# Five broadcasts of the tokens' norms by TensorE: one fp32 product each, or two products of rounded diagonals and their rests; and one token sum moved behind the norm's chain

## The chip, the cores and the metric

The kernel runs on one core of one Trainium2 chip. The time is the device time of one execution of the whole program, in microseconds (us). The trace is one execution of the program taken by the hardware profiler; every start time below counts from the start of its span.

## The reference

Two transformer blocks follow one another on 512 tokens of width 1024, with 16 meta tokens ahead of them, all in fp32. What matters for this change is the norm that stands ahead of each large product:

```python
def rms_norm(x, g):
    xf = x.astype(jnp.float32)
    y = xf * lax.rsqrt(jnp.mean(xf * xf, axis=-1, keepdims=True) + EPS)
    return (y * g.astype(jnp.float32)).astype(x.dtype)
...
hn = rms_norm(h, ffn_norm_g[l])
h = h + (jax.nn.silu(hn @ w_ffn_gate[l]) * (hn @ w_ffn_up[l])) @ w_ffn_down[l]
```

The first block has a windowed attention and an indexed sparse latent attention (its queries pass a norm of 256 entries), gates, an output product and a feed-forward part of 2816. The second has a differential and a windowed attention, gates, an output product and a feed-forward part of the same size. A norm closes each block.

## The kernel before

Activations lie transposed: partitions are features, the 512 tokens are columns. A large product takes a pair of output chunks (`b` = 0 and 1, banks `psL[:, 0]` and `psL[:, 1]`) at a time. Every fp32 weight tile is loaded into `stage`, rounded by ScalarE to float32r (`wh`, line 805) and its rest is made by VectorE (`wl = stage - wh`, line 1250, functions `low` and `low_next`); activations are split into `hn[:, 0]` and `hn[:, 1]` in the same way. TensorE then takes three products for each of the eight chunks `k` of the features: `wh` by high part, `wh` by rest, `wl` by high part (line 2106, function `product`). A product of pair `i`, side `b` starts when the rest of its weights is there (`lo[b]`) and when its bank has been read for pair `i-1` (`ev[b]`).

Each engine runs its own list of instructions in order, written out by hand, and waits on semaphores. The argument `between={(m, k): f}` of `product` puts other TensorE work ahead of chunk `k` of part `m`.

The factor of the norm of a token, 1/rms, is not applied to `hn` before the product but to the product's result, as a tile `R` in which every partition holds the 512 factors. It is made by a chain that crosses two engines:

- TensorE adds the squares over partitions (`sums`, line 2167: products with one column of ones), result in `psT[:, 1, 0:4]`, tokens on partitions; semaphore `ssq_mm`.
- VectorE computes 1/sqrt in one `tensor_scalar` and eight steps on 4 columns (`new_rms`, lines 1698 and 1275 to 1282), and `diagonals` (line 1292) multiplies the identity by the factors of each of the four token blocks: four 128x128 instructions into `diag`; semaphore `diag_ok`.
- TensorE multiplies `diag` by a matrix of ones (`spread_rms`, line 2171), one fp32 product of 512 columns, which puts the factors into every partition of a bank of `psT`; semaphore `bcast`. The trace has two MATMUL records for one fp32 product.
- VectorE copies the bank to `R` (line 1774; 1904 and 1905 in the second block's start), semaphore `R_ok`.

Such a broadcast stands in six places: in `kv1` (`spread_first`), ahead of the latent queries (`spread_second`, inside `product("aq1", 1, 1)`), in each of the two feed-forward parts (`norm_spread`, inside `product("gu1a", 0, 1)` and `product("gu2a", 0, 1)`), and two at once at the start of the second block (`spread_both`, inside `product("kv2", 0, 1)`, ahead of chunk 1 of its second part; the products of kv2 have 264 columns). The second of that pair takes `diag2`, which lies in `tmp[:, 0]`.

In `swiglu` VectorE's order at the first pair of a feed-forward part is

```python
low(name, i, 1)
token_sum(l, 0)
new_rms(head[0])
diagonals(diag, rs[:, 0:4]).then_inc(diag_ok, 1)
low_next(name, i, False)
v.wait_ge(bcast, head[1])
v.tensor_copy(R, psT[:, 1, :]).then_inc(R_ok, 1)
...
v.tensor_tensor(ft[:, 0, :], psL[:, 0, :], R, ALU.mult).then_inc(ev[0], 1)
```

`token_sum(l, 0)` (line 1708) is one 128x1024 subtraction on the normed activations, which ScalarE rounds later and the fast form of the gate products reads in later pairs. The last line (line 1783) frees bank 0 for the product of the second pair. On entry to `aq1`'s last product the bank was freed by `take_scaled("aq1", 0, 1, ...)` (line 1387), which VectorE runs behind `diagonals` and two instructions for the latent queries' rest (line 1468). In `kv2` bank 0's pair is freed by `take_keys` (line 1383), which needs `R`.

Of the kernel before, what the change touches and what calls it, by code (L numbers as in the profile page):

```python
# [21 lines left out]
F32 = mybir.dt.float32  # L22
F32R = mybir.dt.float32r
# [3 lines left out]
ALU = mybir.AluOpType  # L27
AX_X = mybir.AxisListType.X

P = 128  # L30
# [4 lines left out]
NB = SEQ // P  # L35
# [229 lines left out]
def build(nc, t, out):  # L265
    with ExitStack() as ctx:
# [8 lines left out]
        def at(name, shape, offset, dt=F32):  # L275

            n = int(np.prod(shape[1:])) * size[dt]
            assert offset + n <= nc.sbuf_usable_end, (name, offset + n - nc.sbuf_usable_end)
            return nc.alloc_sbuf_tensor_at(name, shape, dt, offset=offset), -(-(offset + n) // 32) * 32

        def keep(name, shape, dt=F32):
            tensor, top[0] = at(name, shape, top[0], dt)
            return tensor
# [5 lines left out]
        wl = keep("wl", [P, 2, NFH * P], F32R)  # L289
        Rk = keep("Rk", [P, NKEY])  # L290
        R = Rk[:, META:NKEY]
        tmp = keep("tmp", [P, 2, SEQ])
        ident = keep("ident", [P, P])
        ones = keep("ones", [P, P])
        gvec = keep("gvec", [P, NROWS])
        bhalf = keep("bhalf", [P, 2 * KD])
        g12 = keep("g12", [P, KD])
# [85 lines left out]
        tail = max(o, ar0 + 4 * (2 * NFH * SEQ + 6 * SEQ + 3 * 4 * SEQ))  # L383
        qT, o = at("qT", [P, 4, SEQ], tail)
        selm, _ = at("selm", [P, NB, NKEY], o, BF16)
        diag, o6 = at("diag", [P, NB, P], o)
        sq, o6 = at("sq", [P, SEQ], o6)
        sqacc, _ = at("sqacc", [P, 2, SEQ], tail)
        hotA, o5 = at("hotA", [BUCKETS + 1, LEN_A], tail)
# [241 lines left out]
        def _(pool):  # L631
# [9 lines left out]
                                        pattern=[[META, NH]], channel_multiplier=-1))  # L641
            own.link(pool.memset(tab[BUCKETS:BUCKETS + 1, :], NEG))
            own.link(pool.memset(st[:, 0, 0:6], 1.0))
            pool.memset(ones[:], 1.0).then_inc(consts, 1)
            pool.wait_ge(consts, 1)
            for tile_ in (cn, ikn, avn):
                pool.memset(tile_[:, MC, :], 0.0)
# [589 lines left out]
        def _(v):  # L1237
# [6 lines left out]
            def low(name, i, b, by_pool=POOL_LOW):  # L1244

                if name in by_pool:
                    return
                v.wait_ge(hi[b], PAIR0[name] + i + 1)
                n = KC[name] * P
                v.tensor_tensor(wl[:, b, 0:n], stage[:, b, 0:n], wh[:, b, 0:n].bitcast(F32), ALU.subtract).then_inc(lo[b], 1)  # L1250
# [18 lines left out]
            def rsqrt(x, y, n, parts=P, done=None):  # L1269
# [16 lines left out]
                else:  # L1286
                    dv.link(ins)

            def diagonals(dst, r):

                for n in range(NB):
                    ins = v.tensor_scalar(dst[:, n, :], ident[:], r[:, n:n + 1], None, ALU.mult)
                return ins
# [166 lines left out]
            v.wait_ge(ssq_mm, 1)  # L1460
            dv.link(v.tensor_scalar(st[:, 7, 0:4], psT[:, 1, 0:4], 1.0 / 256, EPS, ALU.mult, ALU.add))
            rsqrt(st[:, 7, 0:4], rs[:, 0:4], 4)
            diagonals(diag, rs[:, 0:4]).then_inc(diag_ok, 1)

            v.wait_ge(bqhi, 2)
            for k in range(2):
# [228 lines left out]
            def new_rms(ssq_count, n0=0, n1=NB, done=None):  # L1695

                v.wait_ge(ssq_mm, ssq_count)
                dv.link(v.tensor_scalar(st[:, 8, n0:n1], psT[:, 1, n0:n1], 1.0 / D, EPS, ALU.mult, ALU.add))
                rsqrt(st[:, 8, n0:n1], rs[:, n0:n1], n1 - n0, done=done)
# [63 lines left out]
            def swiglu(l, part, head=None):  # L1763
                name, f0, pairs_ = f"gu{l}{'abc'[part]}", before_part(l, part), gate_pairs(l, part)
                first, pair0 = pairs_[0]
                for i in range(first):
                    if i == 0:
                        low(name, i, 1)
                        token_sum(l, 0)
                        new_rms(head[0])  # L1770
                        diagonals(diag, rs[:, 0:4]).then_inc(diag_ok, 1)
                        low_next(name, i, False)
                        v.wait_ge(bcast, head[1])
                        v.tensor_copy(R, psT[:, 1, :]).then_inc(R_ok, 1)
                        v.wait_ge(R_ok, head[1])
                    elif i == 1:
                        token_sum(l, 1)
                    elif i == 2:
                        token_sum_low(l, 1)
                    elif i == 3:  # L1780
                        token_sum_low(l, 3)
                    done(name, i, 0)
                    v.tensor_tensor(ft[:, 0, :], psL[:, 0, :], R, ALU.mult).then_inc(ev[0], 1)  # L1783
                    if i:
                        low_next(name, i, False)
                    opened(i, f0, ft[:, 0, :], ft[:, 1, :])
                    if i == 1:
                        token_sum_low(l, 0)
                        token_sum(l, 2)
                    elif i == 2:  # L1790
                        token_sum(l, 3)
                        token_sum_low(l, 2)
                    elif i == first - 1:
                        weight_sums(name, first, pair0)
                        sum_low(pair0, 0)
                        second_low(name, first)
                    times_up(name, i, 1, i, f0, ft[:, 0, :], (lambda: low(name, i + 1, 1)) if i < first - 1 else None)
                    if i == first - 1:
                        sum_low(pair0, 1)
                    inner_low(i, f0)  # L1800

                for i, n in pairs_:
                    last = i == pairs_[-1][0]
                    done(name, i, 0)
                    v.wait_ge(out_x, 2 * n + 1)
                    v.tensor_tensor(ft[:, 0, 0:HT], psS[:, 1, 0:HT], part_x[:, 0:HT], ALU.add).then_inc(ev[0], 1)
                    low(name, i + 1, 0)
                    low(name, i + 1, 1)
                    v.wait_ge(acc_y, 2 * n + 2)
                    v.wait_ge(out_x, 2 * n + 2)  # L1810
                    dv.link(v.tensor_tensor(ft[:, 0, HT:], psS[:, 2, 0:HT], part_x[:, HT:], ALU.add))
                    v.tensor_tensor(ft[:, 0, :], ft[:, 0, :], R, ALU.mult).then_inc(gate_ok, 1)
                    v.wait_ge(acc_x, 3 * n + 3)
                    v.wait_ge(out_y, n + 1)
                    v.wait_ge(out_z, n + 1)
                    v.tensor_tensor(ft[:, 2, :].rearrange("p (a t) -> p a t", a=2), psS[:, 0, 0:HT].unsqueeze(1).broadcast_to([P, 2, HT]),
                                    part_z[:].rearrange("p (a t) -> p a t", a=2), ALU.add).then_inc(ev[1], 1)
                    v.wait_ge(ev[1], PAIR0[name] + i + 1)
                    v.tensor_tensor(ft[:, 2, :], ft[:, 2, :], R, ALU.mult).then_inc(gate_ok, 1)
                    v.wait_ge(gate_ok, 2 * n + 2)  # L1820
                    opened(i, f0, ft[:, 0, :], ft[:, 1, :])
                    opened(i + 1, f0, ft[:, 2, :], tanh2[:])
                    if not last:
                        weight_sums(name, i + 2, n + 1)
                    times_up(name, i, 0, i + 1, f0, ft[:, 0, :])
                    low_next(name, i + 1, last)
                    if not last:
                        sum_low(n + 1, 0)
                    inner_low(i, f0)
                    if not last:  # L1830
                        sum_low(n + 1, 1)
                    times_up(name, i + 1, 1, i + 1, f0, ft[:, 2, :])
                    if not last:
                        second_low(name, i + 2)
                    elif part == 2:
                        low(f"dn{l}c", 0, 1)
                    inner_low(i + 1, f0)
# [57 lines left out]
            dv.link(v.tensor_scalar(st[:, 9, 0:4], st[:, 9, 0:4], 1.0 / D, EPS, ALU.mult, ALU.add))  # L1895
            rsqrt(st[:, 9, 0:4], rs[:, 4:8], 4)
            dv.link(v.tensor_tensor(rs[:, 8:12], rs[:, 0:4], rs[:, 4:8], ALU.mult))
            diag2 = tmp[:, 0, :].rearrange("p (n c) -> p n c", n=NB)
            diagonals(diag, rs[:, 0:4])
            diagonals(diag2, rs[:, 8:12]).then_inc(diag_ok, 1)  # L1900
            low_next("kv2", 0, False)
            v.wait_ge(bcast, 4)
            v.tensor_copy(Rk[:, 0:META], Rmeta[:, 1, :])
# [181 lines left out]
        def _(pe):  # L2085
# [84 lines left out]
            def spread_rms(bank, d):  # L2170
                return pe.matmul(psT[:, bank, :], ones[:], d.rearrange("p n c -> p (n c)"), start=True, stop=True)


            pe.wait_ge(consts, 1)
            pe.wait_ge(g1_in, 16)
# [67 lines left out]

            def spread_second():
                pe.wait_ge(diag_ok, 2)
                spread_rms(1, diag).then_inc(bcast, 1)

            def logits(t):

# [201 lines left out]
            def layer_rest(l, ssq0, norm):  # L2451
# [16 lines left out]

                def norm_spread():
                    pe.wait_ge(diag_ok, ssq0 + 1)  # L2470
                    spread_rms(1, diag).then_inc(bcast, 1)

                product(name, 0, 0, hn, made=(hg_lo, KD * (2 * l - 2)))
                product(name, 0, 1, hn, between={(0, 1): norm_sums, (0, 6): norm_spread})
# [16 lines left out]

            def spread_both():
                pe.wait_ge(diag_ok, 4)
                spread_rms(0, diag)
                spread_rms(1, tmp[:, 0, :].rearrange("p (n c) -> p n c", n=NB)).then_inc(bcast, 1)

            product("kv2", 0, 0, hn, meta=3, made=(hg_lo, KD), between={(1, 2): sums_of_both})
            product("kv2", 0, 1, hn, meta=1, between={(1, 1): spread_both})
            products("kv2", hn, first=1, meta=1)
            product("qa2", 0, 0, hn)  # L2500
            for b in range(2):
# [186 lines left out]
```

## Time and profile before

| | |
|---|---|
| three runs | 1478.28, 1479.45 and 1480.2 us, median 1479.45 |
| the profiled execution | 1478.32 us, its span 1476.6 us |
| TensorE (PE) busy | 1462.8 us, 99% of the span |
| VectorE (DVE) busy | 957.4 us, 65% |
| ScalarE (ACT) busy | 609.1 us, 41% |
| GpSimd (POOL) busy | 178.9 us, 12% |

A busy matmul includes an end that is modelled: successive MATMUL records of one engine overlap, and the distance of two starts is what one of them takes of the engine. "Idle before, releaser" names the time for which an engine's next instruction waited and what ended the wait.

### The profile page before, as it was taken

The numbers are of one execution on the slowest core, as the hardware profiler recorded it, in microseconds if no ns is written. First come the engines' busy times: TensorE is split into PE (matmuls) and PEld (weight loads), VectorE is DVE, ScalarE is ACT, GpSimd is POOL, SyncE is SP. The second block draws the span as 40 slices with busy tenths as digits, with TensorE's granted clock in tenths as the row PEclk, the third lists the DMA queues.
The fourth block names the chain that finished last, engine by engine and source line by source line (L and its number), as shares of the span: only waits on it lengthen the run. The fifth ranks groups of instructions, "written<-read, shape, count | busy, mean of one in ns | idle before, by whom it ended". The sixth has DMA issues, their size and how long they took to land.

```text
span 1476.6 us, 21866 instructions
## 1 busy us (share of the span) xinstructions
PE 1462.8 (99%) x8042; PEld 1229.8 (83%) x8042; DVE 957.4 (65%) x1736; ACT 609.1 (41%) x1066; POOL 178.9 (12%) x163
## 2 busy tenths in 40 slices
PE   8999999999999999999999999999999999999998
PEld 7867786888888898898898777777888888988987
DVE  6678986575784587387854472524757955873875
ACT  5234446535442343244511364444344423432444
POOL 2013325100000000000003663220000000000000
PEclk9999999999999999999999999999999999999999
DMA  7624320133333333332323202221333333333322
GB/s 178 152 78 144 112 57 1 32 111 99 93 100 95 113 101 86 99 115 74 98 86 85 57 5 82 58 65 36 114 90 96 100 101 114 91 95 100 115 71 101
DMA packets 250325, 132.99 MB, mean 90 GB/s; under 512 B 21241, under 2 KB 247669, under 8 KB 250238
## 3 DMA queue, kind: packets, MB, share of 16 engines
q1 hardware_dynamic: 248014, 123.92, 29.3%
q0 software_dynamic: 2144, 7.77, 1.9%
q8 instruction: 55, 0.90, 0.2%
q14 instruction: 32, 0.26, 0.1%
q10 hardware_dynamic: 80, 0.14, 0.0%
HBM read 129.67 MB, written 6.38 MB: 92 GB/s over the span
## 4 chain that ended last, share of the span: by engine, by line
PE 95%; DVE 2%; ACT 1%; DMA 1%; issue 1%; POOL 0%; DVEq 0%; ACTq 0%; SPq 0%
PE psL L2106 52%; PE psS L2129 12%; PE psL L2292 12%; PE psS L2106 5%; PE psT L2301 2%; PE psL L2427 1%; PE psS L2605 1%; PE psS L2342 1%; PE psL L2560 1%; PE psS L2400 1%; PE psS L2583 1%; PE psS L2531 1%; PE psS L2329 1%; DMA stage<-in_w_out 1%; PE psS L2532 0%
## 5 line engine op out<-in xcount | busy, mean ns | idle before, releaser
L805 ACT ACTIVATE wh<-stage 128x1024 fp32r<-128x1024 f32 (+3 forms) x231 | 224.8, 973 | 381.6 <-PE psL L2106 270.1
L2106 PE MATMUL psL<-hn,wh 128*128 128x512 f32 x1104 | 343.6, 392 | 0.4 <-DVE ft L1783 0.4
L1250 DVE TENSOR_TENSOR wl<-stage,wh 128x1024 fp32r<-128x1024 f32 (+2 forms) x188 | 208.3, 1108 | 77.0 <-ACT wh L805 76.8
L2106 PEld LDWEIGHTS psL<-hn,wh 128*128 128x128 f32 x1104 | 204.7, 188 | 45.7 <-issue 4.8
L2106 PE MATMUL psL<-hn,wl 128*128 128x512 f32 x552 | 215.0, 389 | 0.0
L2106 PE MATMUL psL<-hid,wh 128*128 128x512 f32 x680 | 209.4, 389 | 0.0
L2292 PE MATMUL psL<-hn,wh 128*128 128x512 f32 x496 | 165.0, 414 | 0.2 <-DVE yn L1991 0.2
L2106 PEld LDWEIGHTS psL<-hid,wh 128*128 128x128 f32 x680 | 127.5, 188 | 26.8
L2106 PE MATMUL psL<-hid,wl 128*128 128x512 f32 x340 | 132.3, 389 | 0.0
L2106 PEld LDWEIGHTS psL<-hn,wl 128*128 128x128 f32 x552 | 103.6, 188 | 21.9
L668 POOL TENSOR_TENSOR wl<-stage,wh 128x1024 fp32r<-128x1024 f32 (+1 forms) x43 | 97.5, 2270 | 197.8 <-ACT wh L805 197.8
L2292 PEld LDWEIGHTS psL<-hn,wh 128*128 128x128 f32 x496 | 84.4, 189 | 23.9 <-issue 11.1
L2292 PE MATMUL psL<-hn,wl 128*128 128x512 f32 x248 | 97.8, 394 | 0.0
L1842 DVE TENSOR_TENSOR hT<-hT,psL 128x512 f32 (+1 forms) x46 | 31.6, 686 | 85.3 <-PE psL L2106 85.2
L2106 PE MATMUL psS<-hn,wh 128*128 128x264 f32 x448 | 83.7, 288 | 0.3 <-DVE hn L1300 0.2
L2106 PE MATMUL psL<-mix,wh 128*128 128x512 f32 x256 | 79.8, 393 | 0.3 <-DVE wl L1250 0.2
L2129 PE MATMUL psS<-xt,wsh 128*128 128x256 f32 x432 | 79.3, 283 | 0.0
L2106 PEld LDWEIGHTS psL<-hid,wl 128*128 128x128 f32 x340 | 63.8, 188 | 13.1
L2106 PEld LDWEIGHTS psS<-hn,wh 128*128 128x128 f32 x448 | 70.0, 190 | 2.2 <-issue 1.2
L2129 PEld LDWEIGHTS psS<-xt,wsh 128*128 128x128 f32 x432 | 67.4, 192 | 0.0
L2106 PE MATMUL psS<-hn,wl 128*128 128x264 f32 x224 | 63.8, 285 | 0.0
L2129 PE MATMUL psS<-xt,wsl 128*128 128x256 f32 x216 | 61.1, 283 | 0.0
(443 smaller groups left out, 2565.2 us busy)
## 6 DMA issues: line engine op xcount, KB each, us to landing
stage<-in_w_in SPq DMA_DIRECT2D x53, 512.0 KB, 3.7
stage<-in_w_ffn_gate SPq DMA_DIRECT2D x22, 512.0 KB, 3.7
stage<-in_w_ffn_up SPq DMA_DIRECT2D x22, 512.0 KB, 3.7
stage<-in_w_ff_gate SPq DMA_DIRECT2D x22, 512.0 KB, 3.6
stage<-in_w_ff_up SPq DMA_DIRECT2D x22, 512.0 KB, 3.7
stage<-in_w_out SPq DMA_DIRECT2D x16, 512.0 KB, 3.9
stage<-in_w_ffn_down SPq DMA_DIRECT2D x16, 512.0 KB, 3.9
stage<-in_w_ff_down SPq DMA_DIRECT2D x16, 512.0 KB, 3.9
```

The source lines that it names most:

```text
L668: pool.tensor_tensor(wl[:, b, 0:n], stage[:, b, 0:n], wh[:, b, 0:n].bitcast(F32), ALU.subtract).then_inc(lo[b], 1)
L805: act.activation(wh[:, b, 0:n], stage[:, b, 0:n], ACT.Copy).then_inc(hi[b], 1)
L1250: v.tensor_tensor(wl[:, b, 0:n], stage[:, b, 0:n], wh[:, b, 0:n].bitcast(F32), ALU.subtract).then_inc(lo[b], 1)
L1842: v.tensor_tensor(hT[:, n, :], hT[:, n, :], psL[:, b, :], ALU.add).then_inc(ev[b], 1)
L2106: ins = pe.matmul(dst, w[:, b, k * P:(k + 1) * P], x[:, part, k, c0:c1], start=k + n == 0, stop=k == kc - 1 and n == 2)
L2129: ins = pe.matmul(dst, w[:, cols], x(part, k), start=not add and k + n == 0, stop=k == KD // 2 - 1 and n == 2, skip_group_check=True)
L2292: ins = pe.matmul(psL[:, b, :], w[:, b, k * P:(k + 1) * P], hn[:, part_, k, META:], start=k + n == 0, stop=k == KD - 1 and n == 2)
L2301: ins = pe.transpose(psT[:, n % 2, m * P:(m + 1) * P], tile[:, col:col + P], ident[:])
L2329: pe.matmul(psS[:, 2 * (u % 2), 0:W], aqT[r, h % 4, i * P:(i + 1) * P], akz[r, k0:k0 + W], start=True, stop=True).then_inc(p["s"], 1)
L2342: ins = pe.matmul(psS[:, 2 * (i % 2) + 1, h * HD:(h + 1) * HD], PTa[:, u % 2, n * P:(n + 1) * P], avn[:, c, h // 4 * HD:h // 4 * HD + HD], ...
L2400: ins = pe.matmul(latent_banks(u0 + g)[:, bank, 0:k1 - k0], qT[r, t % 4, i * P:(i + 1) * P], kz[r, t % 4, k0:k1], start=True, stop=True)
L2427: ins = pe.matmul(psL[:, i % 2, h * HD:(h + 1) * HD], PT[:, n % 4, m * P:(m + 1) * P], vB[:, c, h * HD:(h + 1) * HD], start=h == 0 and m = ...
```

## The change

Five of the six broadcasts (all but the one in `kv1`) take two float32r products in place of one fp32 product. `diagonals_split` first writes the four rounded diagonals, and then, behind a wait on the engine's own semaphore, their four rests by `scalar_tensor_tensor` (identity times factor minus the rounded value). The matrix of ones is now made as float32r: a memset of `junk` and a copy behind it. `diag2_r` takes the place of all of `tmp`, and `diag_r` is twice as long as `diag` was. In `swiglu` the first token sum stands behind the diagonals. In `kv2` the two broadcasts stand ahead of chunk 6 of the second part, not ahead of chunk 1.

```diff
-            pool.memset(ones[:], 1.0).then_inc(consts, 1)
+            own.link(pool.memset(junk[:, 0:P], 1.0))
+            pool.tensor_copy(ones_r[:], junk[:, 0:P]).then_inc(consts, 1)
...
+            def diagonals_split(dst, r):
+
+                for n in range(NB):
+                    ins = v.tensor_scalar(dst[:, 0, n, :], ident[:], r[:, n:n + 1], None, ALU.mult)
+                dv.link(ins)
+                for n in range(NB):
+                    ins = v.scalar_tensor_tensor(out=dst[:, 1, n, :], in0=ident[:], scalar=r[:, n:n + 1], in1=dst[:, 0, n, :].bitcast(F32),
+                                                 op0=ALU.mult, op1=ALU.subtract)
+                return ins
...
-            diagonals(diag, rs[:, 0:4]).then_inc(diag_ok, 1)
+            diagonals_split(diag_r, rs[:, 0:4]).then_inc(diag_ok, 1)
...
                         low(name, i, 1)
+                        new_rms(head[0])
+                        diagonals_split(diag_r, rs[:, 0:4]).then_inc(diag_ok, 1)
                         token_sum(l, 0)
-                        new_rms(head[0])
-                        diagonals(diag, rs[:, 0:4]).then_inc(diag_ok, 1)
                         low_next(name, i, False)
...
-            diag2 = tmp[:, 0, :].rearrange("p (n c) -> p n c", n=NB)
-            diagonals(diag, rs[:, 0:4])
-            diagonals(diag2, rs[:, 8:12]).then_inc(diag_ok, 1)
+            diagonals_split(diag_r, rs[:, 0:4])
+            diagonals_split(diag2_r, rs[:, 8:12]).then_inc(diag_ok, 1)
...
+            def spread_split(bank, d):
+                for part in range(2):
+                    ins = pe.matmul(psT[:, bank, :], ones_r[:], d[:, part].rearrange("p n c -> p (n c)"), start=part == 0, stop=part == 1)
+                return ins
...
-                spread_rms(1, diag).then_inc(bcast, 1)
+                spread_split(1, diag_r).then_inc(bcast, 1)
...
-            product("kv2", 0, 1, hn, meta=1, between={(1, 1): spread_both})
+            product("kv2", 0, 1, hn, meta=1, between={(1, 6): spread_both})
```

## Rows read from the trace of the kernel before

**Rows 1.** The page: TensorE's clock in 40 slices, and all engines' busy time

```profile
PE 1462.8 (99%) x8042; PEld 1229.8 (83%) x8042; DVE 957.4 (65%) x1736; ACT 609.1 (41%) x1066; POOL 178.9 (12%) x163
...
PEclk9999999999999999999999999999999999999999
```

**Rows 2.** Waits of TensorE: waiter, releaser; us in total, times, longest

```profile
PE psL L2106 <- DVE ft L1783: 0.4, 2, 0.2
```

**Rows 3.** Timeline of TensorE in gu1a: start, length, engine, line, operation

```profile
381.33 0.39 PE L2106 MATMUL psL<-hn,wl 128*128 128x512 f32 x1
...
382.01 0.39 PE L2106 MATMUL psL<-hn,wl 128*128 128x512 f32 x1
...
383.55 0.40 PE L2106 MATMUL psL<-hn,wl 128*128 128x512 f32 x1
...
384.25 0.40 PE L2106 MATMUL psL<-hn,wl 128*128 128x512 f32 x1
384.86 0.70 PE L2106 MATMUL psL<-hn,wh 128*128 128x512 f32 x2 [0.22 <-DVE ft L1783]
385.39 0.39 PE L2106 MATMUL psL<-hn,wl 128*128 128x512 f32 x1
```

**Rows 4.** Timeline of VectorE in gu1a

```profile
376.67 1.22 DVE L1708 TENSOR_TENSOR ta<-hg 128x1024 f32<-128x1024 f32 x1
378.94 0.16 DVE L1698 TENSOR_SCALAR st<-psT 128x4 f32<-128x4 f32 x1 [1.05 <-PE psT L2167]
...
380.72 0.88 DVE L1292 TENSOR_SCALAR diag<-ident,rs 128x128 f32<-128x128 f32 x4
381.52 1.22 DVE L1250 TENSOR_TENSOR wl<-stage,wh 128x1024 fp32r<-128x1024 f32 x1
383.30 0.69 DVE L1774 COPY Rk<-psT 128x512 f32<-128x512 f32 x1 [0.56 <-PE psT L2171]
384.02 0.69 DVE L1783 TENSOR_TENSOR ft<-psL,Rk 128x512 f32<-128x512 f32 x1
```

**Rows 5.** Timeline of both engines around `spread_second`

```profile
82.36 1.41 DVE L1468 SCALAR_TENSOR_TENSOR bqg<-bqT,gvec,bqg 128x512 fp32r<-128x512 f32 x2
...
83.68 0.68 DVE L1387 SCALAR_TENSOR_TENSOR aqT<-psL,Rk 128x512 f32<-128x512 f32 x1
...
84.28 0.36 DVE L1481 SCALAR_TENSOR_TENSOR acc<-relu,iwn,causal 128x144 f32<-128x144 f32 x1
...
84.89 0.62 PE L2106 MATMUL psL<-hn,wh 128*128 128x512 f32 x2
...
87.15 1.02 PE L2171 MATMUL psT<-diag,ones 128*128 128x512 f32 x2
```

**Rows 6.** Timeline of both engines around `spread_both` in kv2

```profile
737.12 0.87 DVE L1292 TENSOR_SCALAR tmp<-ident,rs 128x128 f32<-128x128 f32 x4
...
737.41 0.28 PE L2106 MATMUL psS<-hn,wl 128*128 128x264 f32 x1
...
740.07 0.17 DVE L1903 COPY Rk<-Rmeta 128x16 f32<-128x16 f32 x1 [0.94 <-PE psT L2171]
740.11 0.28 PE L2106 MATMUL psS<-hn,wl 128*128 128x264 f32 x1
...
741.47 0.71 DVE L1383 TENSOR_TENSOR kaT<-psS,Rk 128x528 f32<-128x528 f32 x1
...
742.30 0.28 PE L2106 MATMUL psS<-hn,wl 128*128 128x264 f32 x1
```

**Rows 7.** Timeline of TensorE at the start of the program

```profile
3.06 0.25 PE L2176 MATMUL psT<-ident,rows 8*128 8x8 f32 x1 [3.06 <-POOL ones L644]
4.62 1.97 PE L2199 MATMUL psL<-ident,xin 128*128 128x128 f32 x8 [1.31 <-DMA xin<-in_x]
```

**Rows 8.** Windows: length, busy us and instructions of each engine, PEclk, DMA, GB/s

```profile
9.00:12.00 3.00, 2.32 (x17) 1.98 (x16) 2.96 (x6) 3.00 (x7) 0.39 (x1) 0.83 1.11 353
12.00:13.90 1.90, 1.90 (x10) 1.68 (x9) 1.86 (x4) 1.90 (x6) 1.90 (x4) 0.50 0.38 68
```

More of the change, by code:

```diff
@@ L291, in build @@
         R = Rk[:, META:NKEY]
+        diag2_r, _ = at("diag2_r", [P, 2, NB, P], top[0], F32R)
         tmp = keep("tmp", [P, 2, SEQ])
         ident = keep("ident", [P, P])
-        ones = keep("ones", [P, P])
+        ones_r = keep("ones", [P, P], F32R)
+        ones = ones_r[:].bitcast(F32)
         gvec = keep("gvec", [P, NROWS])
@@ L385, in build @@
         selm, _ = at("selm", [P, NB, NKEY], o, BF16)
-        diag, o6 = at("diag", [P, NB, P], o)
+        diag, _ = at("diag", [P, NB, P], o)
+        diag_r, o6 = at("diag_r", [P, 2, NB, P], o, F32R)
         sq, o6 = at("sq", [P, SEQ], o6)
@@ L2470, in norm_spread @@
                     pe.wait_ge(diag_ok, ssq0 + 1)
-                    spread_rms(1, diag).then_inc(bcast, 1)
+                    spread_split(1, diag_r).then_inc(bcast, 1)
                 product(name, 0, 0, hn, made=(hg_lo, KD * (2 * l - 2)))
@@ L2493, in spread_both @@
                 pe.wait_ge(diag_ok, 4)
-                spread_rms(0, diag)
-                spread_rms(1, tmp[:, 0, :].rearrange("p (n c) -> p n c", n=NB)).then_inc(bcast, 1)
+                spread_split(0, diag_r)
+                spread_split(1, diag2_r).then_inc(bcast, 1)
             product("kv2", 0, 0, hn, meta=3, made=(hg_lo, KD), between={(1, 2): sums_of_both})
-            product("kv2", 0, 1, hn, meta=1, between={(1, 1): spread_both})
+            product("kv2", 0, 1, hn, meta=1, between={(1, 6): spread_both})
             products("kv2", hn, first=1, meta=1)
```

## The prediction

> **What bounds the kernel now.** I read the page first. TensorE is busy for 99% of the span and its granted clock is full in all 40 slices, while VectorE stands at 65% [rows 1]. So a microsecond taken off TensorE's own work is worth a microsecond, and so is each one for which TensorE is made to wait; an average of 65% on VectorE says nothing about one chain on it. The second view was the list of TensorE's waits. The reader is to see that TensorE already waits for the line just behind a broadcast (line 1783, the first product by `R`), twice [rows 2], once in each feed-forward part. Then I read the timelines of both engines around each of the five places.
>
> **What two rounded products save.** In gu1a a group of three rounded products takes 382.01 - 381.33 = 0.68 us, 0.227 us each [rows 3]. The group with the broadcast in it takes 383.55 - 382.01 = 1.54 us, so the fp32 broadcast takes 0.86 us of TensorE. Two rounded products of the same 512 columns take 0.45. The saving is 0.41 us a place, 2.0 us for five. The bounds: nothing, if a product by ones cost what an fp32 pass does (0.43), and 0.41; I take 0.41, since the same form of product stands 0.68 us beside it.
>
> **What the split costs on VectorE.** The four `tensor_scalar` stay (0.88 us together [rows 4]). Added are a wait on the engine's own semaphore and four `scalar_tensor_tensor` of 128 columns. None of this size is in the trace. The nearest takes 0.36 us for 144 columns [rows 5], and 16 columns fewer make about 0.345. Two instructions of this kind in a row, with no wait between them, end 1.41 us after the first begins [rows 5]; the second starts some 0.67 us behind the first, so an instruction begins about 0.07 us before the one ahead ends, and the step is 0.27. The gap of a wait is 383.30 + 0.69 to 384.02, 0.03 us [rows 4]. Estimate: 0.03 + 3 x 0.27 + 0.345 = 1.19 us a split, both until its semaphore and until the next instruction. Bounds: the step of the `tensor_scalar`, (0.88 - 0.28) / 3 = 0.20, gives 0.82; four that each wait for the one before, 4 x 0.40, give 1.6.
> The Trainium skill ("VectorE: DVE Perf Modes", the section on the TRN2 errata) says that each SBUF-source instruction pays a fixed latency, so many small tiles lose most, which speaks against four more small ones; its table gives 58 cycles plus one per column, 0.194 us at 0.96 GHz. By that figure the four add about 0.78 us, and the whole forecast would be some 2 us lower; the row of 0.36 us for 144 columns is well above its 0.21.
>
> **gu1a and gu2a.** Before, the token sum (1.22 us) ran from 376.67 to 377.89 and VectorE then stood idle for 1.05 us until TensorE's sums came, so the norm's chain starts at 378.94 in any order [rows 4]: ahead of the chain the token sum was free. Behind it, it is not. The new order by these rows:
> - the rounded diagonals end at 381.60, the rests at 382.79;
> - TensorE comes to the broadcast at 382.24, waits until about 382.85, runs 0.45 us and loses 0.1 on restarting: it is at the end of side 1 (two groups of 0.68 further) at about 384.75. Before it was there at 384.25 + 0.23 = 384.48;
> - token sum 382.71 to 383.93, then the rest of the next weights (`low_next`) 383.97 to 385.18, then the copy to `R` from 385.11 (the broadcast is long done), then line 1783 from 385.83 to 386.52.
>
> TensorE needs line 1783 for pair 1, and took it up 0.15 us after it ended: 384.86, with a pair that was 0.70 long instead of 0.61 [rows 3, 4]. It now takes it up at 386.67. The shift is 1.81 us. The same as a sum: token sum 1.26, split 1.19, less the 0.64 for which VectorE used to wait for the broadcast. The saving of 0.41 vanishes in TensorE's wait, which grows from about 0.4 to about 1.9. What is queued behind: ScalarE's tanh, the product for side 1 and all of the pair, all of which wait for line 1783 anyway and move with it. SP's load for pair 2 is issued behind `low_next`, 2.4 us later, and its slot is wanted only at the end of a product of 5.5 us; I cost it at nothing. Two places: +3.6 us, bounds +2.9 and +4.4 by the step.
>
> **kv2.** The last of the two diagonals ended at 737.99 [rows 6]. With two splits in the chain it is 740.37. The broadcasts' new place is five chunks further on; a chunk is (742.30 - 740.11) / 6 = 0.365 us, so TensorE is there at 737.53 + 1.82 = 739.35 and waits 1.05 us, instead of some 0.5 before. Four rounded products and the restart take 1.0, and the bank is whole, with its modelled tail, at about 741.6. Before it was at 740.03. From the first copy (740.07) to the end of `take_keys` (741.47 + 0.71 = 742.18) are 2.11 us, all in a row [rows 6]; now they run from 741.64 to 743.75. TensorE, which took up the next product at 742.30 + 0.12 = 742.42 without waiting, has only two chunks of cover left, arrives at 742.15 and starts at about 744.0 with the restart: +1.6 us. In other words, the later place keeps the diagonals' lateness off TensorE and pays it back at `take_keys`. Bounds: +0.9 and +2.4.
>
> **spread_second.** The broadcast itself stands at 87.15, the diagonals were done before 82.44 [rows 5], so no wait there and 0.41 is saved. But `take_scaled` (83.68, ends 84.36) is behind the diagonals on VectorE and frees the bank for TensorE's product at 84.89 [rows 5]: a cover of 0.53 less 0.15 for the semaphore. With 1.19 more it ends at 85.55, and TensorE starts at 85.70 and loses 0.09 on restarting: +0.9. Net +0.5, bounds +0.1 and +0.9.
>
> **The start.** The matrix of ones is two GpSimd instructions, so the first transpose at 3.06 comes some 0.35 us later (one more short instruction and a wait; none of GpSimd's shown is dearer at this size); it is 0.25 long, and TensorE then waited for x until 4.62 [rows 7]. That 1.31 us hides it: 0. With the cover gone it would be 0.35.
>
> **Sum.** 0.5 + 3.6 + 1.6 = +5.7 us. The profiled execution, 1478.32 us (1476.6 of span, 1.7 around it), becomes 1484.0. It lay 1.1 us below the median of the runs, so against the median: 1485.1 us. Terms at their bounds give 0.1 + 2.9 + 0.9 = 3.9 and 0.9 + 4.4 + 2.4 = 7.7, so 1483.3 to 1487.2, and the runs spread by about 1 us either way.
>
> **Rivals.**
> - *The chain hides after all* (not slower). VectorE has slack where I see none, and only TensorE's side is left: -2.0 us, 1477.4; if the two waits for line 1783 went too, 1476.5. It decides at one point, whether line 1783 ends by 384.33 (TensorE's arrival 384.48 less 0.15). It already ended 0.4 us later than that, and 1.8 is put ahead of it. Chance 0.07.
> - *Half is given back.* A later wait of TensorE in the pairs that follow shrinks because everything it waits for did not shift, weights from memory above all. The rows show no wait of TensorE for a weight load, so little is there to give back. About 1482. Chance 0.1.
> - *Rounded by ones is no cheaper than an fp32 pass* (the change doesn't do what it says). The feed-forward places do not move, since VectorE sets them; spread_second and kv2 get 0.4 and 0.8 dearer: 1486.3. Against it stand the steps of rows 3. Chance 0.03.
> - *The clock falls in the longer waits.* From 9 to 12 us, where TensorE was busy for 2.32 of 3 us with short transposes and waits, the granted clock went to 0.83 of full, and then to 0.50 for 1.9 us [rows 8]: about 2.9 us at the lower level, 1.5 us lost. If each of the three waits of 1 to 2 us brought that on, +4.5: 1489.6. Against it: those waits lie between dense products. The Trainium skill ("TensorE: Matmul & The Clock Gate", the section on HAM oscillation) warns that idle gaps between bursts of matmuls bring the 1.2 GHz level back; rows 8 show the level, no row here shows a lone gap doing it. Chance 0.04.
>
> **How the numbers follow.** My case has 0.76. The range is 1482.0 to 1488.0: the bounds of the terms with 1 us of spread below and above, which takes in the third rival and half of the second; outside are the first, the fourth and the rest, under 0.2. A measurement can tell about 0.2%, 3.0 us, from no change. Slower by more than that (above 1482.4) are my case, the third and fourth rivals and a little of the second: 0.84. Within it are most of the second, and the first where the two waits stay: 0.12. Faster needs more than the whole saving of 2.0: 0.04.
>
> **What the profile after would show.** The product at line 2106 that opens pair 1 of gu1a and gu2a idles some 1.7 to 2 us for line 1783, `take_keys` becomes a releaser of TensorE (about 1.6 us), and `take_scaled` in aq1 one with about 0.7. The broadcast's records are 0.39 long and 0.23 apart. The rests are about 0.345 long, 0.27 apart. In gu1a the broadcast waits about 0.5 us for the rests. I am wrong if the rests take under 0.15 us apiece, if the copy to `R` begins within 1 us of the broadcast in gu1a, or if the added idle time in these four places sums to less than 3 us.

## The result and the profile after

The changed kernel takes 1484.53 us (median of 7 runs, 1484.19 to 1485.44); the kernel before takes 1479.45 (7 runs, 1478.28 to 1481.19). The ratio is 1.0033, 95% interval 1.0024 to 1.0043: slower by 5.1 us, where 5.7 was forecast. The profiled execution of the changed kernel has a span of 1482.4 us against 1476.6.

First the page: busy time, share of the span and instructions of each engine.

```profile
PE 1463.0 (99%) x8042; PEld 1231.6 (83%) x8042; DVE 963.0 (65%) x1756; ACT 609.2 (41%) x1066; POOL 179.2 (12%) x164
```

Beside [rows 1] VectorE has 20 instructions and 5.6 us more, at an unchanged share of 65%. TensorE's share stays at 99% too, though its idle time (span less busy time) went from 13.8 to 19.4 us. Where the loss lies the page doesn't say. The waits of TensorE do (waiter, releaser; us in total, times, longest):

```profile
PE psL L2119 <- DVE ft L1797: 3.4, 2, 1.7
...
PE psT L2188 <- DVE diag_r L1299: 1.6, 3, 0.9
PE psS L2119 <- DVE kaT L1397: 1.5, 1, 1.5
...
PE psL L2119 <- DVE aqT L1401: 0.6, 1, 0.6
```

Line 1797 is line 1783 of before, 1397 is `take_keys` and 1401 `take_scaled`. The first wait was 0.4 us in all [rows 2], the last two were not in the list, and the second was one of 0.4 in kv2. The new waits name the four places of the forecast. (The 3.4 us for `ones` and 1.0 us for x, which are in the list too, belong to the start of the program.)

The instructions on the split diagonals (duration in ns, least, median and most):

```profile
L1296 DVE TENSOR_SCALAR diag_r<-ident,rs x20: 277/281/288, 82.0 to 1124.2; 128x128 fp32r<-128x128 f32 x20
L1299 DVE SCALAR_TENSOR_TENSOR diag_r<-ident,rs,diag_r x20: 341/344/352, 82.9 to 1125.3; 128x128 fp32r<-128x128 f32 x20
...
L2188 PE MATMUL psT<-diag_r,ones x10: 393/398/502, 88.4 to 1126.1; 128*128 128x512 f32 x10
```

One of the four instructions that make the rests takes 0.344 us (0.345 was estimated from the 144-column row).

gu1a, VectorE's timeline (start, length, engine, line, operation), beside [rows 4]:

```profile
379.49 0.16 DVE L1712 TENSOR_SCALAR st<-psT 128x4 f32<-128x4 f32 x1 [2.11 <-PE psT L2180]
...
381.27 0.88 DVE L1296 TENSOR_SCALAR diag_r<-ident,rs 128x128 fp32r<-128x128 f32 x4
382.18 1.14 DVE L1299 SCALAR_TENSOR_TENSOR diag_r<-ident,rs,diag_r 128x128 fp32r<-128x128 f32 x4
383.23 1.22 DVE L1722 TENSOR_TENSOR ta<-hg 128x1024 f32<-128x1024 f32 x1
384.49 1.23 DVE L1254 TENSOR_TENSOR wl<-stage,wh 128x1024 fp32r<-128x1024 f32 x1
385.63 0.69 DVE L1788 COPY Rk<-psT 128x512 f32<-128x512 f32 x1
386.35 0.69 DVE L1797 TENSOR_TENSOR ft<-psL,Rk 128x512 f32<-128x512 f32 x1
```

and TensorE's, beside [rows 3]:

```profile
382.63 0.39 PE L2119 MATMUL psL<-hn,wl 128*128 128x512 f32 x1
383.37 0.73 PE L2188 MATMUL psT<-diag_r,ones 128*128 128x512 f32 x2 [0.35 <-DVE diag_r L1299]
...
385.09 0.39 PE L2119 MATMUL psL<-hn,wl 128*128 128x512 f32 x1
387.18 0.70 PE L2119 MATMUL psL<-hn,wh 128*128 128x512 f32 x2 [1.71 <-DVE ft L1797]
```

The idle time of VectorE ahead of the chain went from 1.05 to 2.11 us: that is the token sum's old place, now empty. Behind the diagonals VectorE has no idle time at all until line 1797 is done, and TensorE stands for 1.71 us. The broadcast, cheaper by half, was over at about 384.1 and nobody was waiting for it: the copy to `R` began at 385.63.

kv2, TensorE and then VectorE, beside [rows 6]:

```profile
741.92 0.28 PE L2119 MATMUL psS<-hn,wl 128*128 128x264 f32 x1
743.09 1.21 PE L2188 MATMUL psT<-diag_r,ones 128*128 128x512 f32 x4 [0.88 <-DVE diag_r L1299]
...
744.75 0.28 PE L2119 MATMUL psS<-hn,wl 128*128 128x264 f32 x1
746.49 0.51 PE L2119 MATMUL psS<-hn,wh 128*128 128x264 f32 x2 [1.46 <-DVE kaT L1397]
```

```profile
741.89 1.14 DVE L1299 SCALAR_TENSOR_TENSOR diag_r<-ident,rs,diag_r 128x128 fp32r<-128x128 f32 x4
742.95 1.22 DVE L1254 TENSOR_TENSOR wl<-stage,wh 128x1024 fp32r<-128x1024 f32 x1
744.33 0.18 DVE L1916 COPY Rk<-Rmeta 128x16 f32<-128x16 f32 x1 [0.17 <-PE psT L2188]
...
745.73 1.32 DVE L1397 TENSOR_TENSOR kaT<-psS,Rk 128x528 f32<-128x528 f32 x2
```

And `spread_second`, both engines, beside [rows 5]:

```profile
85.27 0.68 DVE L1401 SCALAR_TENSOR_TENSOR aqT<-psL,Rk 128x512 f32<-128x512 f32 x1
...
86.09 0.70 PE L2119 MATMUL psL<-hn,wh 128*128 128x512 f32 x2 [0.64 <-DVE aqT L1401]
...
88.42 0.62 PE L2188 MATMUL psT<-diag_r,ones 128*128 128x512 f32 x2
...
88.88 0.63 PE L2119 MATMUL psL<-hn,wh 128*128 128x512 f32 x2
```

The granted clock (the number behind POOL's) stays at full speed in the stretches that hold the two kinds of long wait, although TensorE is busy for 0.49 of 2.2 and 0.54 of 2 us there:

```profile
385.00:387.20 2.20, 0.49 (x4) 0.10 (x2) 2.00 (x3) 0.13 (x1) 0.00 (x0) 1.00 0.06 13
...
745.00:747.00 2.00, 0.54 (x5) 0.51 (x5) 1.97 (x5) 1.06 (x1) 0.00 (x0) 1.00 0.64 186
```

**One table for all kernels.** The time of a whole run differs by 1 to 2 us between executions of one kernel, so each place was also measured by itself, between two events of TensorE in the profiled execution. *second*: from the first index logits (before: 80.25) to the first product of uq1 (93.00). *gu1a, gu2a*: from the start of the norm's sums to the last product of the first chunk of pair 1 (before: 377.88 to 385.39). *kv2*: the same (before: 730.20 to 742.66). *Run* is the median less that of the kernel before in the same session.

| kernel | second | gu1a | gu2a | kv2 | run |
|---|---|---|---|---|---|
| before | 12.75 | 7.51 | 7.51 | 12.46 | 0 |
| after | 13.25 | 9.22 | 9.22 | 13.95 | +5.1 |
| e1 token sum ahead | 13.24 | 8.03 | 8.02 | 13.95 | +2.2 |
| e2 kv2 ahead of chunk 1 | 13.26 | 9.22 | 9.23 | 15.54 | +5.5 |
| e3 token sum behind, fp32 | 12.75 | 8.04 | 8.05 | 12.45 | +0.9 |
| e4 no rests | 12.36 | 8.04 | 8.04 | 12.79 | +0.5 |
| e5 no rests, old places | 12.37 | 7.12 | 7.12 | 12.57 | -2.1 |
| e6 placed | 12.36 | 7.26 | 7.23 | 12.10 | -1.5 |
| e7 as e2, again | 13.24 | 9.22 | 9.23 | 14.04 | one run |
| e8 kv2 ahead of chunk 4 | 13.26 | 9.22 | 9.22 | 13.95 | one run |
| e9 take_scaled first | 12.37 | 9.23 | 9.23 | 14.31 | +4.1 |

### The profile page after: what moved, and what is told of

The parts are those of the page before. It is cut to its first block, busy times and chain, and to the rows that moved or that the text cites. A ratio compares the mean times of both kernels' runs of the same rounds, so it can differ in the third digit from the quotient of the medians.

```text
span 1482.4 us, 21887 instructions
## 1 busy us (share of the span) xinstructions
PE 1463.0 (99%) x8042; PEld 1231.6 (83%) x8042; DVE 963.0 (65%) x1756; ACT 609.2 (41%) x1066; POOL 179.2 (12%) x164
## 4 chain that ended last, share of the span: by engine, by line
PE 94%; DVE 3%; issue 1%; DMA 1%; ACT 1%; POOL 0%; SPq 0%; ACTq 0%; DVEq 0%
PE psL L2119 52%; PE psL L2310 12%; PE psS L2142 12%; PE psS L2119 5%; PE psT L2319 2%; PE psL L2445 1%; PE psS L2623 1%; PE psS L2360 1%; PE psL L2578 1%; PE psS L2418 1%; PE psS L2601 1%; PE psS L2549 1%; PE psS L2347 1%; PE psS L2550 0%; PE psS L2332 0%
```

## The experiments

**e1, the token sum's place in the changed kernel.**

```diff
+                        token_sum(l, 0)
                         new_rms(head[0])
                         diagonals_split(diag_r, rs[:, 0:4]).then_inc(diag_ok, 1)
-                        token_sum(l, 0)
```

> The changed kernel with the first token sum back ahead of the norm's chain, all else as changed. My theory (the token sum was free in VectorE's idle time and costs its 1.26 us behind the chain, twice): 2.5 us less than the changed kernel, about 1482.0 (+2.5 on the kernel before); TensorE's wait for the first product by R in gu1a and gu2a falls from 1.7 us to about 0.5 each, and VectorE idles about 1.05 us ahead of the chain. Rival, the token sum's place is neutral and the four rests alone make the wait: 1484.5 and waits of 1.7.

Measured: 1481.26 us, ratio to the kernel before 1.0016 (1.0007 to 1.0025): 2.2 us over it, where the changed kernel is 5.1 over it. By place 1.2 us less in gu1a and in gu2a, nothing elsewhere: 2.4 us. VectorE in gu1a:

```profile
377.58 1.22 DVE L1722 TENSOR_TENSOR ta<-hg 128x1024 f32<-128x1024 f32 x1
379.85 0.16 DVE L1712 TENSOR_SCALAR st<-psT 128x4 f32<-128x4 f32 x1 [1.05 <-PE psT L2180]
...
383.59 1.22 DVE L1254 TENSOR_TENSOR wl<-stage,wh 128x1024 fp32r<-128x1024 f32 x1
384.73 0.68 DVE L1788 COPY Rk<-psT 128x512 f32<-128x512 f32 x1
385.45 0.69 DVE L1797 TENSOR_TENSOR ft<-psL,Rk 128x512 f32<-128x512 f32 x1
```

The token sum is back in idle time, of which 1.05 us is left, as before. The rival (the place is neutral) has fallen; what is left in each feed-forward part, 0.5 us, is the split.

**e2, the broadcasts' place in kv2.**

```diff
-            product("kv2", 0, 1, hn, meta=1, between={(1, 6): spread_both})
+            product("kv2", 0, 1, hn, meta=1, between={(1, 1): spread_both})
```

> The changed kernel with the two broadcasts of kv2 back ahead of chunk 1. My theory (the end of the diagonals on VectorE sets when R is there, wherever TensorE waits for them): the same time within 0.2 us, with the waits moved: about 2.7 us for the rests at the broadcasts and almost none for take_keys. Rival, the later place is what costs: 1.5 us less. Rival, the later place hides the rests: 1.8 us more.

Measured: 1484.53 us, ratio 1.0034 (1.0021 to 1.0048), so no difference that the runs can tell. But in the profiled execution the place is 1.6 us longer than the changed kernel's, against my expectation. TensorE's timeline, and the windows from there (length, busy us of PE, PEld, DVE, ACT, POOL, granted clock, DMA share, GB/s):

```profile
743.03 1.25 PE L2188 MATMUL psT<-diag_r,ones 128*128 128x512 f32 x4 [2.70 <-DVE diag_r L1299]
744.08 0.64 PE L2119 MATMUL psS<-hn,wh 128*128 128x264 f32 x2
744.51 0.42 PE L2119 MATMUL psS<-hn,wl 128*128 128x264 f32 x1
```

```profile
743.00:745.00 2.00, 1.97 (x9) 1.78 (x10) 1.79 (x3) 0.00 (x0) 0.00 (x0) 0.75 0.00 0
745.00:747.00 2.00, 2.00 (x11) 2.00 (x11) 1.39 (x3) 0.00 (x0) 0.00 (x0) 0.50 0.73 211
```

Behind a wait of 2.70 us TensorE ran at half its clock (1.2 GHz) for about 3.4 us, from 744.0 on: a chunk took 0.66 us, not 0.36, and the next product could not begin when `take_keys` allowed it. So the early place is not neutral in every execution. Whether the wait brought the fall on, one execution doesn't show; e7 and e8 take this up.

**e3, the order alone.** The kernel before, fp32 broadcasts, with the token sum behind the diagonals.

```diff
-                        token_sum(l, 0)
                         new_rms(head[0])
                         diagonals(diag, rs[:, 0:4]).then_inc(diag_ok, 1)
+                        token_sum(l, 0)
```

> The kernel before (fp32 broadcasts) with the token sum behind the diagonals and nothing else changed. My theory: VectorE's chain grows by the token sum's 1.26 us less the 0.64 us for which it waited for the broadcast, so +0.6 us in each of two places, +1.2 us in all, about 1480.7. Rival, the full 1.26 each: +2.5. Rival, the place is neutral: 0.

Measured: 1479.99 us, ratio 1.0006 (0.9997 to 1.0015), which by itself can't be told from nothing. By place +0.53 and +0.54 us, as by the list of waits:

```profile
PE psL L2106 <- DVE ft L1783: 1.5, 2, 0.7
```

1.5 us instead of 0.4 [rows 2]. The chain had 0.64 us of slack against the fp32 broadcast, and that pays for half of the token sum.

**e4, the rests.** This kernel leaves the four rests out; both of TensorE's products take the rounded diagonals.

```diff
-                dv.link(ins)
-                for n in range(NB):
-                    ins = v.scalar_tensor_tensor(out=dst[:, 1, n, :], in0=ident[:], scalar=r[:, n:n + 1], in1=dst[:, 0, n, :].bitcast(F32),
-                                                 op0=ALU.mult, op1=ALU.subtract)
...
-                    ins = pe.matmul(psT[:, bank, :], ones_r[:], d[:, part].rearrange("p n c -> p (n c)"), start=part == 0, stop=part == 1)
+                    ins = pe.matmul(psT[:, bank, :], ones_r[:], d[:, 0].rearrange("p n c -> p (n c)"), start=part == 0, stop=part == 1)
```

> The changed kernel without the four rests on VectorE (and without the wait ahead of them); TensorE's second product takes the rounded diagonals again, so the factors are twice too large, and TensorE's work is that of the changed kernel. By my sum: spread_second -0.4, gu1a and gu2a +0.6 each (token sum behind the chain), kv2 +0.35 (take_keys has two chunks of cover only): +1.2 on the kernel before, about 1480.6, 3.9 us less than the changed kernel. Rival, the rests are cheap and the places are what costs: within 1 us of 1484.5.

Measured: 1479.57 us, ratio 1.0007 (0.9998 to 1.0016), 0.5 us over the kernel before, which by itself can't be told from nothing, and so 4.6 us under the changed one. By place -0.39, +0.53, +0.53 and +0.33: +1.0 us on the kernel before, where +1.2 was expected. So the rests are what the split costs, 1.2 us in each of gu1a and gu2a behind a late token sum.

**e5, TensorE's side alone.** e4 with the token sum ahead of the chain and kv2's broadcasts ahead of chunk 1.

> Two rounded products in all five places, without the rests on VectorE (TensorE takes the rounded diagonals twice, so the factors are twice too large), the token sum ahead of the norm's chain and the broadcasts of kv2 ahead of chunk 1: TensorE's side of the change alone, with the order of before. My theory (TensorE's saving is real and is lost only because VectorE's chain pays for it): spread_second -0.4, gu1a and gu2a -0.45 each (set by low_next and line 1783 on VectorE, no longer by the broadcast), kv2 -0.8: 2.1 us less than the kernel before. Rival, a product by ones costs as much as an fp32 pass: no difference.

Measured: 1477.24 us, ratio 0.9987 (0.9978 to 0.9996): 2.1 us less than before, as expected, and the rival (no difference) has fallen. By place -0.38, -0.39 and -0.39. kv2 shows +0.11 in the profiled execution instead of -0.8, and the clock says why:

```profile
732.00:734.00 2.00, 2.00 (x14) 2.00 (x13) 1.66 (x11) 0.00 (x0) 0.00 (x0) 0.67 0.88 244
734.00:736.00 2.00, 2.00 (x11) 2.00 (x11) 1.66 (x11) 0.97 (x1) 0.00 (x0) 0.50 0.11 30
736.00:738.00 2.00, 2.00 (x18) 2.00 (x18) 2.00 (x9) 0.09 (x1) 0.00 (x0) 0.97 0.00 0
```

The clock fell to half at 732.7, about 3 us after the sixteen one-column sums had begun (729.78), and stayed there for some 3.4 us. The four places add up to -1.05 us in this execution, so the 2.1 of the medians, whose interval is 0.6 to 3.3 us, does not confirm the -0.8 of kv2. What TensorE itself saves there shows in its timeline at full clock, first e5 and then before:

```profile
738.64 1.08 PE L2184 MATMUL psT<-diag_r,ones 128*128 128x512 f32 x4
...
739.80 0.29 PE L2115 MATMUL psS<-hn,wl 128*128 128x264 f32 x1
```

```profile
738.04 1.12 PE L2171 MATMUL psT<-diag,ones 128*128 128x512 f32 x2 [0.36 <-DVE tmp L1292]
```

From the first broadcast to the same product of `wl` are 1.16 us in e5 and 740.11 - 738.04 = 2.07 before [rows 6]: 0.9 us less for two broadcasts and a restart.

**e6, only what pays.** The kernel before with: the split and the rounded products in `spread_second` alone, `take_scaled` of aq1 ahead of that norm's chain; fp32 elsewhere, with

```diff
-                product(name, 0, 1, hn, between={(0, 1): norm_sums, (0, 6): norm_spread})
+                product(name, 0, 1, hn, between={(0, 1): norm_sums, (0, 5): norm_spread})
...
-            product("kv2", 0, 1, hn, meta=1, between={(1, 1): spread_both})
+            product("kv2", 0, 1, hn, meta=1, between={(1, 2): spread_both})
...
-            v.tensor_copy(R, psT[:, 1, :])
-            v.tensor_copy(tmp[:, 1, :], psT[:, 0, :]).then_inc(R_ok, 1)
+            v.tensor_copy(R, psT[:, 1, :]).then_inc(R_ok, 1)
...
                 take_keys("kv2", i, 0, keys[2 * i])
+                if i == 0:
+                    dv.link(v.tensor_copy(tmp[:, 1, :], psT[:, 0, :]))
```

> The kernel before, with what the theory says pays and nothing else: the split and the two rounded products in spread_second alone, with take_scaled of aq1 moved ahead of the diagonals there; fp32 broadcasts elsewhere, one chunk earlier in gu1a and gu2a (ahead of chunk 5, where the diagonals have just ended) and one later in kv2 (chunk 2, where TensorE no longer waits for them), and in kv2 the copy of the second bank behind take_keys, 0.6 us off its chain. Expected: spread_second -0.4, gu1a and gu2a -0.3 each, kv2 -0.36: 1.3 to 1.4 us less than the kernel before. If VectorE's chains did not set these places, only the -0.4 would show.

Measured: 1477.87 us, ratio 0.9992 (0.9983 to 1.0001), 1.5 us less than before; the interval just reaches 1, so the gain rests on the places. By place -0.39, -0.25, -0.28 and -0.36, together -1.3, as expected. In gu1a TensorE no longer waits for VectorE, neither at the broadcast for more than its restart nor behind it:

```profile
380.43 0.39 PE L2120 MATMUL psL<-hn,wl 128*128 128x512 f32 x1
380.74 1.12 PE L2185 MATMUL psT<-diag,ones 128*128 128x512 f32 x2
...
384.25 0.39 PE L2120 MATMUL psL<-hn,wl 128*128 128x512 f32 x1
384.48 0.62 PE L2120 MATMUL psL<-hn,wh 128*128 128x512 f32 x2
```

**e7, e2 once more.**

> The kernel of e2 (the changed kernel with the broadcasts of kv2 ahead of chunk 1) once more, to see whether the fall of TensorE's clock behind its wait of 2.7 us comes again. If the lone wait brings it on: granted clock at 0.5 for some 3 us behind the broadcasts, chunks of kv2 0.66 us long instead of 0.36. If it was chance: 1.0 throughout, and the place as in the changed kernel to 0.1 us.

Measured: one run, 1484.36 us (kernel before 1479.26). This time the clock fell ahead of the broadcasts, behind the sums (granted 0.69 of full from 735 to 739 us), TensorE came to the broadcasts 1.5 us later and had only 1.19 us to wait:

```profile
742.47 1.21 PE L2188 MATMUL psT<-diag_r,ones 128*128 128x512 f32 x4 [1.19 <-DVE diag_r L1299]
743.52 0.41 PE L2119 MATMUL psS<-hn,wh 128*128 128x264 f32 x2
743.76 0.29 PE L2119 MATMUL psS<-hn,wl 128*128 128x264 f32 x1
```

Behind it the clock was full, and kv2 took 14.04 us, the changed kernel's 13.95 to 0.1: with the clock undisturbed behind the wait, the place was neutral in this execution. My question to this run, whether a lone wait of 2.7 us brings the clock down each time, has no answer, since there was no such wait.

**e8, the broadcasts ahead of chunk 4.**

> The changed kernel with the broadcasts of kv2 ahead of chunk 4: a wait of 0.88 + 2 x 0.36 = 1.6 us for the rests, take_keys waiting about 0.7. By VectorE's chain the next product starts where it does in the changed kernel, to 0.1 us; granted clock 1.0 if only the longer wait of e2 brings it down.

Measured: one run, 1484.16 us; kv2 13.95, to 0.01 that of the changed kernel. TensorE waited 0.74 us for `take_keys` and hardly at all at the broadcasts, because here too the clock fell behind the sums (granted 0.57 of full from 735 to 739 us) and TensorE came late. So the place held, though not through the waits that I expected, and the run says nothing on a wait of 1.6 us at the broadcasts.

**e9, the queue behind the split in aq1.**

```diff
+            take_scaled("aq1", 0, 1, aqT[:, 1, :], R, QSCALE)
             v.wait_ge(ssq_mm, 1)
...
                                        op0=ALU.mult, op1=ALU.subtract).then_inc(bqlo, 1)
-            take_scaled("aq1", 0, 1, aqT[:, 1, :], R, QSCALE)
```

> The changed kernel with take_scaled of aq1 moved ahead of the second norm's chain on VectorE, nothing else. My theory (take_scaled was the only thing that the split delayed there): TensorE's wait of 0.64 us for it goes, spread_second's stretch is 0.9 us shorter than in the changed kernel and 0.4 shorter than before the change. Time about 1483.6. Rival, TensorE waits for a later piece of VectorE's work instead: 0.

Measured: 1483.35 us, ratio 1.0028 (1.0017 to 1.0039). *second* is 12.37, 0.88 less than in the changed kernel and 0.38 less than before; TensorE's wait for `take_scaled` is gone. What made the split dear there was one instruction in VectorE's queue that had nothing to do with the norm. (kv2's 14.31 in this execution has the fall of the clock behind the sums in it: TensorE came to the broadcasts when the diagonals were already made, and the place is 0.36 us longer than in the changed kernel.)

## Why the prediction was right

The forecast was +5.7 us; by place the profile gives 0.50 + 1.71 + 1.71 + 1.49 = +5.4, the runs +5.1. Each of the three terms came out within 0.2 us, so the sum is not a matter of errors that cancel. None of the three signs of being wrong appeared: the rests take 0.34 us apiece, the copy to `R` in gu1a begins 2.3 us behind the start of the broadcast, and the added idle time of TensorE in the four places is 6.3 us.

- **What two rounded products save**: right. e5 has -0.38 and -0.39 us in the three places with one broadcast (0.41 forecast), and 0.9 us on TensorE for the two of kv2. Its median of -2.1 us agrees, though the clock's fall in kv2 makes the exact match in part luck.
- **What the split costs**: right, 1.14 us for the four rests and 0.03 for the wait, 1.19 forecast. By the table of the Trainium skill ("VectorE: DVE Perf Modes", the section on the TRN2 errata) the four would have taken an estimated 0.78 us; the measurement decides for the row of this trace. e4, without the rests, is 0.89 + 1.18 + 1.18 + 1.16 = 4.4 us shorter over the four places than the changed kernel, and 4.6 by the medians.
- **gu1a and gu2a**: the mechanism right, the size 1.71 against 1.81. (The wait that "grows from about 0.4 to about 1.9" counts the restart and the semaphore; the trace puts it at 0.22 and 1.71.) The two causes were separated: the token sum's place costs 1.2 with the split (after against e1) and 0.53 without it (e3 against before), the split 1.2 behind a late token sum and 0.52 with an early one. They are one chain: the first to be added uses up its 0.64 us of slack, the second is paid in full. SP's later load cost nothing: from 387.2 to 430 us TensorE waits for nothing in the changed kernel, as in e1.
- **kv2**: the mechanism right, +1.49 against +1.6; the waits 0.88 and 1.46 against 1.05 and 1.6. e7 and e8 show that VectorE's chain sets the end wherever the broadcasts stand, in e7 even when TensorE comes 1.5 us late to them; at chunk 6 the slack is smaller, and in e9 TensorE's lateness cost 0.36 us. The step that the later place "pays it back" holds where the clock is undisturbed behind the broadcasts (e7); e2's profile shows that the early place can cost 1.6 us more.
- **spread_second**: right, +0.50 against +0.5; e9 shows that `take_scaled` was the whole of it.
- **The start**: right as to cause. The first transpose came at 3.39 instead of 3.06 and the wait for x fell to 0.99 us. The copy to `R` of the first broadcast was at 27.32 against 26.90, but at 27.13 in e3, which has the old matrix of ones, and at 26.76 in e6, which has the new one: these 0.4 us are a matter of the execution. The two profiled spans differ by 5.9 us, the ends of TensorE's last products by 5.4.
- **The rivals**: that the chain hides is refuted by the waits and e4. That half is given back: the runs lie 0.3 us under the sum by place, less than they can tell, and no later wait of TensorE shrank in gu1a's pairs. That rounded products are no cheaper: refuted by e5. The clock: it did not fall behind the changed kernel's waits of 1.7 and 1.5 us in the profiled executions; it did behind the 2.7 us of e2, once. The fall that this rival was priced by [rows 8] cost TensorE some 1.5 us of work but the kernel nothing that shows: the first copy to `R` came at 26.90 in before and between 26.76 and 27.43 in e1, e3, e6 and e8, where the clock did not fall there. Between dense products it did cost time, 1.6 us in e2.

## What to carry to other kernels

Halving an operation on the busiest engine is worth its price only where the engine that prepares it has slack up to the point where the busiest engine needs it again: follow the preparing engine's queue to that point, not to the operation. Here 0.41 us saved by a broadcast cost 1.2 us of VectorE in a chain with 0.64 us of slack or less, and of the places tried it paid only where the delayed instruction could be moved ahead (-0.39 us). Work that stands in idle time ahead of a chain is free there; behind it, it costs what the chain's slack doesn't cover: the token sum of 1.26 us cost 0.53 with the slack (e3) and 1.2 without.

## What the runs showed of the hardware that was not expected

- A lone wait of 2.70 us between dense products was followed by about 3.4 us at 1.2 GHz (e2, the one profile with such a wait); no profile showed it behind the waits of 1.71 us (after, e2, e7, e8, e9) and of about 1.5 us (after, e1, e4, e9). The Trainium skill ("TensorE: Matmul & The Clock Gate", the section on HAM oscillation) describes the return to 1.2 GHz in waits of about 3 to 5 us for a DMA between short bursts of matmuls. The wait of e2 was shorter than those and stood alone, and since the clock also fell with no long wait near it (below), one execution doesn't show that the wait was the cause.
- Behind the sixteen one-column sums of kv2 the clock fell to half for some 3.4 us in four of the profiled executions (e5, e7, e8, e9) and did not in the others (before, after, e1, e2, e3, e4, e6), with no long wait near it. TensorE counts as busy there. What brings it on in one execution and not in the next stays open. In the kernels with the split it cost 0.0, 0.1 and 0.4 us (e8, e7, e9), since VectorE's chain was longer or nearly so; e5, without the rests, came out 0.9 us above its forecast for kv2.
